# Attention heads on one Trainium2 core: score, value and transpose blocks of TensorE grouped behind every second half unit, and the two softmax maps combined with one pass less

## What is computed

```
q = rmsnorm(q.reshape(b, l, ATTN_HEADS, 2, ATTN_HEAD_DIM), q_norm) * (ATTN_HEAD_DIM ** -0.5)
k = rmsnorm(k.reshape(b, l, ATTN_HEADS, 2, ATTN_HEAD_DIM), k_norm)
...
    s = jnp.einsum('bqhtd,bkhtd->bhtqk', qb, k).astype(jnp.float32) + bias[None, :, None]
    pr = jax.nn.softmax(s, axis=-1)
    attn = pr[:, :, 0] - lam * pr[:, :, 1]
    return jnp.einsum('bhqk,bkhe->bqhe', attn.astype(v.dtype), v)
...
o = rmsnorm(o, subln) * (1.0 - lam_init)
o = o.reshape(b, l, ATTN_V_DIM) * jax.nn.silu(z)
return o @ w_out
```

## Time and profile before

| what | value |
|---|---|
| median of three runs | 848.48 us (846.72 to 849.82) |
| the profiled execution | 852.42 us |
| its span, first to last instruction | 850.7 us |
| mean granted clock of TensorE in it | 0.982 |
| PE busy | 787.7 us, 93% |
| DVE, POOL, ACT busy | 63%, 54%, 48% |
| attention layer | from about 537 to 851 us |

### The profile page before, as it was taken

The page is one execution under the profiler, slowest core; times in us unless marked ns, Lnnn a source line. Parts: engine busy times, 40 slices in busy tenths (PEclk is TensorE's granted clock), DMA queues, the critical chain, the costliest instruction groups (busy, mean ns, idle before and its releaser), DMA issues.

```text
span 850.7 us, 11488 instructions
## 1 busy us (share of the span) xinstructions
PE 787.7 (93%) x3824; PEld 639.4 (75%) x3824; DVE 538.0 (63%) x893; ACT 405.0 (48%) x807; POOL 456.5 (54%) x254
## 2 busy tenths in 40 slices
PE   1987999999999899999799999899999999998887
PEld 0766888887878788888687888766777777776576
DVE  4754869596777859596662113367668677676732
ACT  4557273634637282745732134344645454645420
POOL 5438494856667475857545434645545636445111
PEclk9999899999999999999999999999999999999999
DMA  9115524324243424233152332513223132120002
GB/s 263 54 41 166 186 62 125 115 73 159 75 148 99 148 58 152 87 111 113 50 198 76 105 99 62 155 51 96 69 77 97 50 97 91 53 96 25 1 1 99
DMA packets 98804, 82.57 MB, mean 97 GB/s; under 512 B 5152, under 2 KB 87424, under 8 KB 96712
## 3 DMA queue, kind: packets, MB, share of 16 engines
q1 hardware_dynamic: 95760, 66.99, 26.4%
q10 hardware_dynamic: 2904, 15.01, 4.8%
q0 software_dynamic: 96, 0.02, 0.0%
HBM read 79.74 MB, written 2.26 MB: 96 GB/s over the span
## 4 chain that ended last, share of the span: by engine, by line
PE 51%; DVE 21%; issue 11%; POOL 8%; ACT 6%; DMA 1%; DVEq 1%; ACTq 0%; SPq 0%; POOLq 0%
PE bank L1259 42%; DVE c_acc L937 4%; POOL w_lo L472 3%; DVE rows L962 3%; POOL stat L464 2%; ACT ex L790 2%; PE bank L1342 2%; DVE sbias L1126 2%; PE bank L1331 1%; PE bank L1355 1%; POOL rows L504 1%; DVE tmp L997 1%; DVE ex L1137 1%; ACT qkvz L855 1%; ACT w_hi L601 1%
## 5 line engine op out<-in xcount | busy, mean ns | idle before, releaser
L472 POOL TENSOR_TENSOR w_lo<-w_raw,w_hi 128x1024 fp32r<-128x1024 f32 x104 | 260.9, 2510 | 256.4 <-ACT w_hi L601 256.3
L1259 PE MATMUL bank<-hn_hi,w_hi 128*128 128x512 f32 (+1 forms) x392 | 160.1, 408 | 11.1 <-DVE xT L952 7.7
L1259 PE MATMUL bank<-hn_hi,w_lo 128*128 128x512 f32 (+1 forms) x392 | 154.5, 394 | 0.0
L1259 PE MATMUL bank<-hn_lo,w_hi 128*128 128x512 f32 (+1 forms) x392 | 154.3, 394 | 0.0
L601 ACT CAST w_hi<-w_raw 128x1024 fp32r<-128x1024 f32 x104 | 108.8, 1047 | 77.1 <-PE bank L1259 70.7
L1259 PE MATMUL bank<-w_hi,hn_hi 128*128 128x512 f32 x320 | 131.4, 410 | 7.7 <-DVE zT L952 5.0
L1259 PE MATMUL bank<-w_hi,hn_lo 128*128 128x512 f32 x320 | 125.6, 392 | 0.0
L1259 PE MATMUL bank<-w_lo,hn_hi 128*128 128x512 f32 x320 | 125.6, 392 | 0.0
L937 DVE SCALAR_TENSOR_TENSOR c_acc<-bank,par,c_acc 128x510 f32<-128x510 f32 (+1 forms) x128 | 95.8, 748 | 34.1 <-ACT c_acc L643 25.4
L790 ACT ACTIVATE ex<-sbias,stat 128x512 f32<-128x512 f32 x64 | 45.7, 716 | 120.6 <-DVE stat L1130 120.6
L1259 PEld LDWEIGHTS bank<-hn_hi,w_hi 128*128 128x128 f32 (+1 forms) x392 | 74.2, 189 | 29.2 <-issue 14.0
(11 more groups left out here) (191 smaller groups left out, 1265.1 us busy)
## 6 DMA issues: line engine op xcount, KB each, us to landing
w_raw<-in_ssd_w_in SPq DMA_DIRECT2D x48, 512.0 KB, 4.0
w_raw<-in_attn_w_in SPq DMA_DIRECT2D x64, 256.0 KB, 3.1
rows<-acs_rows ACTq DMA_DIRECT2D x14, 1024.0 KB, 6.4
w_raw<-in_ssd_w_out SPq DMA_DIRECT2D x16, 512.0 KB, 3.6
w_raw<-in_attn_w_out SPq DMA_DIRECT2D x16, 256.0 KB, 3.1
wbias<-bias_rows SPq DMA_DIRECT2D x8, 448.0 KB, 4.1
rows<-in_x SPq DMA_DIRECT2D x4, 512.0 KB, 5.4
rows<-acs_rows SPq DMA_DIRECT2D x2, 1024.0 KB, 5.9
```

The source lines that it names most:

```text
L472: nc.gpsimd.tensor_tensor(w_lo[:, s, :], w_raw[:, s, :], f32(w_hi[:, s, :]), ALU.subtract)\
L1259: ins = T.matmul(dst, a[i], b[j], start=first and n == 0, stop=last and n == 2)
```

## The change

Three things are changed, all in the attention heads.

1. PE's pieces are regrouped: P, scores 2, `o_sq` back, `probs_t` 1; P; P, scores 3, `probs_t` 2; P, q/k; P, scores 0, `o_nat`, `probs_t` 3; P; P, scores 1, values, `probs_t` 0; P. Three of the eight half units are followed directly by the next one, the last of a head among them. The pieces of ACT and DVE are moved along with them; POOL's and SP's are not. `fills` loses an entry at an odd step.
2. `combine` no longer multiplies the second map in a pass of its own. It works out one factor for each row, minus lambda times the first map's sum over the second's, and adds the second map times this factor to the unscaled first. The result is larger than before by the first map's row sum, and since the head's output is normalised afterwards, this cancels but for the epsilon.
3. So the row sums of the first map are kept for each query block (columns from `SUM0`), and the epsilon of the output norm is multiplied by the square of the sum, in one more small operation on DVE.

```
-                own(V.reciprocal(stat[:, 44:46], stat[:, 40:42]))
-                own(V.tensor_scalar(ex[:, 1, :], ex[:, 1, :], stat[:, 45:46], lam, ALU.mult, ALU.mult))
-                V.scalar_tensor_tensor(am[:, q % 2, :], ex[:, 0, :], stat[:, 44:45], ex[:, 1, :],
-                                       ALU.mult, ALU.subtract).then_inc(a_done, 1)
+                total = stat[:, SUM0 + par_ * NC + q:SUM0 + par_ * NC + q + 1]
+                own(V.reciprocal(stat[:, 45:46], stat[:, 41:42]))
+                own(V.tensor_scalar(stat[:, 46:47], stat[:, 45:46], total, neg_lam, ALU.mult, ALU.mult))
+                V.scalar_tensor_tensor(am[:, q % 2, :], ex[:, 1, :], stat[:, 46:47], ex[:, 0, :],
+                                       ALU.mult, ALU.add).then_inc(a_done, 1)
...
                     if has(3):
+                        total = stat[:, SUM0 + one * NC:SUM0 + (one + 1) * NC]
+                        V.scalar_tensor_tensor(stat[:, 88:92], total, EPS, total, ALU.mult, ALU.mult)
                         dve.wait_ge(o_sqd, it - 2)
                         own(V.reduce_sum(stat[:, 56:60], o_sq[:, :, :], axis=AXX))
-                        V.tensor_scalar(stat[:, 48:52], stat[:, 56:60], 1.0 / SEG, EPS, ALU.mult, ALU.add)\
-                            .then_inc(o_ms, 1)
+                        V.scalar_tensor_tensor(stat[:, 48:52], stat[:, 56:60], 1.0 / SEG, stat[:, 88:92],
+                                               ALU.mult, ALU.add).then_inc(o_ms, 1)
```

PE's `stage_ops` after (the helpers hold the transposes as they were):

```
+                if s == 0:
                     if has(2):
-                        scores(it - 2, 3)
...
+                        scores(it - 2, 2)
+                    if has(3):
+                        o_natural(it - 3)
+                    if has(2):
+                        probs_t(it - 2, 1)
+                if s == 2 and has(2):
+                    scores(it - 2, 3)
+                    probs_t(it - 2, 2)
+                if s == 3 and has(1):
+                    qk_channels(it - 1)
+                if s == 4:
                     if has(1):
...
+                        scores(it - 1, 0)
+                    if has(3):
+                        o_channels(it - 3)
                     if has(2):
-                        probs_t(it - 2, 2)
...
+                        probs_t(it - 2, 3)
+                if s == 6:
+                    if has(1):
+                        scores(it - 1, 1)
                     if has(2):
-                        values(it - 2, pb)
+                        values(it - 2, half)
                     if has(1):
                         probs_t(it - 1, 0)
...
-            fills = [(AH, s) for s in (0, 1, 2, 4, 6)] + [(AH + 1, 1)]
+            fills = [(AH, s) for s in (0, 2, 4, 6)] + [(AH + 1, s) for s in (0, 2)]
```

## The result

| | before | after |
|---|---|---|
| time, us (median; 4 runs each, beside each other) | 849.15 (846.72 to 852.39) | 864.29 (861.65 to 867.54) |
| ratio, 95% interval | | 1.0179 (1.0143 to 1.0214) |
| profiled execution: its span | 850.7 | 859.9 |
| first q/k transposes to the end of the span | 300.0 | 314.5 |

What follows compares the result with a forecast made beforehand. PE's queue sets the pace (busy 32.4 of 33 us). Heads 3 to 7 +8.2, heads 1 and 2 -0.5, after the projections +4.8, small terms +1: +13.5 on 848.48 gives 862.0, range 857 to 868.

Steps and rivals of the forecast that it cites:

- the likeliest case: The main forecast for the whole kernel: 862.0 us, own range 857 to 868, chance 0.71.
- Borders: PE's switches between projections, scores, values and transposes in a head get cheaper: -0.2 a head, -1.5 for all.
- Evacuation: PE waits for ACT's `qkvz` copies after step 7: +1.03 at heads 3 to 7, +2.0 at the first output unit.
- q/k transposes: PE waits because `w_lo` holds DVE's q/k multiplication: +1.15 at each of five heads, +2.0 after the projections.
- The wait for `qT_lo`: PE's wait at scores 0 shrinks with the cheaper combination and one T less: -0.35 a head.
- The tail: First output matmul to the end: +2.0 for q/k transposes, -1.2 for scores 0, +1 exponentials, +1 clock; +2.8 together.
- the exponentials: In the tail, exponentials 1 stand behind `aT_hi` 0, making the last head's scores and combination later: +1, between -1 and +2.
- The clock: In the tail, longer idle stretches of PE keep its clock at the lower level longer: +1, between 0 and 3.
- the third rival: The clock falls in every head of the loop, five times 1.5 more: 869.5 us, chance 0.06.
- The small unplaced term: Small terms not placed, such as maximum L1130 held when step 0's `w_lo` is late, 0.2 a head: +1.

Runs made afterwards that it cites:

- the best kernel: Kernel before in its old order, with the new combination and POOL's `w_lo` of step 2 behind the maximum of scores 3: 837.12 and 837.24 us.
- both causes out: Changed kernel with values and transposes 0 back behind step 7's projections, and step 2's `w_lo` behind the q/k multiplication: 846.01 us, ratio 0.9964.
- the reduction early: Changed kernel with DVE's `probs_lo` 1 back behind the reduction of the squares: 862.32 us, ratio 1.0159.
- the hold moved one step down: Changed kernel with POOL's `w_lo` of step 2 started only when the q/k multiplication is done: 858.81 us, ratio 1.0115.
- the hold off the chain: Changed kernel with POOL's `w_lo` of step 2 started only when the maximum of scores 3 is out: 861.07 us, ratio 1.0153.

## Why the prediction was right, and where its steps were off

The forecast was 862.0, the result 864.29; inside the own range of the likeliest case, with the mechanisms named. Costs are read here from start to start, as the prediction did, and not from the idle times in brackets. By its steps:

- *Borders, -0.2 a head: right, as near as the runs can tell.* The old order without waits has a period of 32.67 (the best kernel), the one with both causes out 33.07. Three small waits stand in that: 0.26 for `qT_lo` (the P ahead of scores 0 takes 3.20 for 2.94; the profile names 0.18), 0.13 for `o_nat` (next point) and 0.16 ahead of the q/k transposes, which the profile doesn't name. They start 0.15 behind the end of the maximum, as they do where it is named (their P takes 3.02, and 2.86 where nothing waits). Without these the period is 32.5, and so is the changed kernel's without its own (35.52 less 1.21, 1.44, 0.25 and 0.13 of the points below). PE in that kernel, with DVE's maximum ahead of the q/k transposes:

```profile
666.12 0.50 PE L1257 MATMUL bank<-qT_hi 64*128 64x512 f32 x2
...
667.02 0.66 PE L1490 MATMUL bank<-ident,o_sq 128*128 128x128 f32 x4
667.51 0.60 PE L1474 MATMUL bank<-ident,am 128*128 128x128 f32 x4
...
676.40 1.32 DVE L1130 TENSOR_SCALAR stat<-stat 128x2 f32<-128x2 f32 x1
...
677.87 1.06 PE L1504 MATMUL bank<-ident,qkvz 128*128 128x128 f32 x8
```

  Scores ahead of T take 0.90 to the next start, as ahead of P, and the T behind them 0.49 where a T ahead of another T takes 0.44 behind P: a border of 0.05, where P behind scores costs 0.13. So the single instance of the earlier trace rows holds in every head. The rule that the prediction weighed (the Trainium skill, TensorEngine Tiling (Array Packing), Key Properties: a change of the tiling mode drains TensorE) would, as the prediction read it, give 0 a head. No run shows that. The regrouped borders are worth 1.0 to 1.4 us in the whole kernel, by an estimate from 0.15 to 0.2 a head and seven heads.
- *A wait I had not seen: 0.13 a head for `o_nat`.* Its transposes stand directly behind scores 0 now. DVE writes it from 722.24 to 723.36, and PE takes it up at 723.41 (the rows of after above), 1.03 behind the scores' start and not 0.90. The prediction has no term for it. The profile names no wait there; only the distance of two starts shows it.

```profile
722.24 1.12 DVE L1194 SCALAR_TENSOR_TENSOR o_nat<-bank,stat,gate 128x128 f32<-128x128 f32 x4
```

- *Evacuation, +1.03 a head and +2.0 at the output units: right, a little small.* Measured 1.21 and 2.3 (the wait went from 0.35 to 2.67). I took from the earlier trace rows the distance of two starts less one matmul of 0.23; the first matmul behind the wait takes 0.34 to the next start (738.00 to 738.34), which is over half of what was missing.
- *q/k transposes, +1.15 a head and +2.0 behind the projections: right in the mechanism, too small in the loop.* Measured 1.44 a head, and from the first output matmul to the transposes 15.57 against a predicted 15.6. The reason (`w_hi` ready, so `w_lo` first) is shown by the run that delays `w_hi`. The missing 0.3 is in the start of the reduction: I had it at +3.3 and the power's end at +7.7, and the power ended at +8.0, because the maximum of scores 2 was held (0.70 for 0.17). How much of the 1.44 is due to which part has no single answer: with the reduction early 0.84 are left, with the hold moved one step down 0.36, and with the hold off the chain nothing.
- *The wait for `qT_lo`, -0.35: right.* The P ahead of scores 0 took 3.60 and takes 3.19, so -0.41.
- *The tail: predicted +2.8, measured +1.6.* The run with the regrouping alone parts it: from the first output matmul to the end it takes 84.65, so the regrouping costs 1.7 there, where I had 2.0 for the transposes, 1 for the exponentials and 1 for the clock, and the cheaper combination gives 0.1 and not 1.2 (in the old order it gave 3.0). The transposes account for the 1.7 (1.9 measured), so the +1 for the exponentials behind `aT_hi` 0 is not seen. Two terms that were too large, of opposite sign, have partly cancelled: that the sum of the tail came out near is luck.
- *The clock.* From the first output matmul to the last block of them, by window, before and after (columns as in the earlier trace rows):

```profile
767.00:830.00 63.00, 53.47 (x250) 40.66 (x248) 37.20 (x88) 24.89 (x51) 19.35 (x10) 0.92 0.03 9
```

```profile
775.00:841.00 66.00, 53.17 (x246) 40.44 (x246) 35.36 (x91) 23.72 (x48) 18.61 (x10) 0.90 0.03 9
```

  By the prediction's own reckoning that is 0.08 x 63 / 0.5 = 10.1 us at the lower level before and 0.10 x 66 / 0.5 = 13.2 after; half the difference, 1.5, is lost. +1 was about the size, as far as two figures with two digits can say (each is good to about 0.6 us here). But the tail grew by no more than its transposes account for, so this part either lay under waits or was won back elsewhere in the tail, and which of the two stays open. The stalls in the loop drew no fall (1.00), so the third rival is out.
- *The small unplaced term, +1: there, and larger.* It was put down for a held maximum when the `w_lo` of step 0 is late. That is what happened to the maximum of scores 2, and its 0.3 a head is the part that the q/k term lacked.

The terms of one head add to 1.21 + 1.44 - 0.41 - 0.2 + 0.13 = 2.17, and the period grew by 2.14. The prediction had 1.65: right in each sign, and too small in the two large ones.

## What to carry to other kernels

When blocks are merged to have fewer breaks, look first at what the moved blocks were covering: here 3.1 us of values and transposes hid an evacuation, and the borders that were saved are worth 0.2 a head against stalls of 2.7. Where two engines' operations are released within a microsecond of each other and one of them can hold the other, find out which comes first and where it would stand if it were late; delaying the one off the path may be the gain. Read the cost of a wait from the distance of two starts, since the idle time that the profile names was 0.1 to 0.3 less here, and small waits had no name at all. An edit's worth belongs to the order it stands in: measure it in both.

## What the runs showed of the hardware

- A DVE operation on two or four columns is held for as long as a large one: 1.32 and 1.14 for 0.17 on 128x2, 2.07 and 1.86 for about 0.15 on 128x4, each beside POOL's `w_lo`, which kept its 2.4. That whoever issues first gets the ports to SBUF which DVE and POOL share, and that the other is blocked, is what the Trainium skill says (SBUF — State Buffer, Who interferes with whom). The runs agree: the margin was 0.17 in the changed kernel.
- POOL's power does not hold DVE, though it too reads and writes SBUF. It ran from 710.45 to 713.35 in the changed kernel, and `am`, with two inputs in SBUF, took its usual 0.75 inside it, where the same operation took 1.66 beside POOL's `v_lo` (the combination alone, 710.53):

```profile
710.80 0.75 DVE L1136 SCALAR_TENSOR_TENSOR am<-ex,stat 128x512 f32<-128x512 f32 x1
```

- The stages ahead took up to 5.3 us more or less from one profiled execution to another in the six kernels whose code is the same up to there. Two spans alone would have given +9.2 for this change and not the 15 of the medians.
